# GpSimd forms S5's rotated states itself, and the read-out takes two products of each turn

## What is computed

```python
bu_r = jnp.einsum('bsgc,gpc->bsgp', ug, bbar_r)
bu_i = jnp.einsum('bsgc,gpc->bsgp', ug, bbar_i)
# x[s] = abar * x[s-1] + bu[s], complex, along the sequence
_, _, xr, xi = lax.associative_scan(_complex_affine_combine, ...)
y = (jnp.einsum('bsgp,gcp->bsgc', xr, c_re) - jnp.einsum('bsgp,gcp->bsgc', xi, c_im) + d_skip * ug)
y = jax.nn.gelu(y)
return y * jax.nn.sigmoid(y @ w_glu + b_glu)
```

## Time and profile before

| | |
|---|---|
| Median of 3 runs | 1662.81 us (1662.75 to 1663.93) |
| The profiled execution | 1659.71 us |
| Its span, first to last instruction | 1657.9 us |
| PE busy | 1551.6 us (94%) |
| VectorE (DVE) busy | 1259.0 us (76%) |
| ScalarE (ACT) busy | 1043.8 us (63%) |
| GpSimd (POOL) busy | 62.8 us (4%) |
| DMA | 469.68 MB, mean 283 GB/s |

### The profile page before, as it was taken

The page is one execution under the profiler, slowest core; times in us unless marked ns, Lnnn a source line. Parts: engine busy times, 40 slices in busy tenths (PEclk is TensorE's granted clock), DMA queues, the critical chain, the costliest instruction groups (busy, mean ns, idle before and its releaser), DMA issues.

```text
span 1657.9 us, 22266 instructions
## 1 busy us (share of the span) xinstructions
PE 1551.6 (94%) x7619; PEld 1202.9 (73%) x7620; DVE 1259.0 (76%) x1719; ACT 1043.8 (63%) x1374; POOL 62.8 (4%) x90
## 2 busy tenths in 40 slices
PE   4899989999897888999999999999999999999997
PEld 2545468887764456888888888888888888888885
DVE  6896345443646237989989989989989989989987
ACT  3105444443425626778778778778778778778775
POOL 5251000000000000000000000000000000000000
PEclk9999999999888988999999999999999999999999
DMA  9635855545654837999999999999999999999970
GB/s 319 232 102 195 313 203 200 177 156 177 228 181 150 307 116 265 365 332 358 365 328 364 362 331 366 350 334 362 354 335 363 351 338 362 351 337 364 353 260 27
DMA packets 203752, 469.68 MB, mean 283 GB/s; under 512 B 5108, under 2 KB 11558, under 8 KB 203574
## 3 DMA queue, kind: packets, MB, share of 16 engines
q1 hardware_dynamic: 202656, 466.80, 77.9%
q0 software_dynamic: 400, 1.09, 0.3%
q10 hardware_dynamic: 646, 1.16, 0.2%
HBM read 467.98 MB, written 1.05 MB: 283 GB/s over the span
## 4 chain that ended last, share of the span: by engine, by line
PE 78%; DVE 6%; ACT 5%; issue 2%; DMA 0%; DVEq 0%; ACTq 0%
PE ps L783 22%; PE ps L785 21%; PE ps L784 21%; PE ps L789 2%; PE ps L1330 2%; DVE w_lo L1882 2%; PE ps L1289 2%; PE ps L1056 1%; ACT work L1778 1%; PE ps L808 1%; ACT w_hi L1548 1%; ACT uT L1561 1%; PE ps L828 1%; PE ps L1204 0%; PE ps L1399 0%
## 5 line engine op out<-in xcount | busy, mean ns | idle before, releaser
L1882 DVE TENSOR_TENSOR w_lo<-ring,w_hi 128x1024 fp32r<-128x1024 f32 (+2 forms) x576 | 667.4, 1192 | 116.3 <-ACT w_hi L1548 102.5
L1548 ACT ACTIVATE w_hi<-ring 128x1024 fp32r<-128x1024 f32 (+2 forms) x576 | 594.9, 1038 | 210.3 <-PE ps L785 206.7
L783 PE MATMUL ps<-w_hi,e_hi 128*128 128x512 f32 x896 | 356.6, 398 | 9.7 <-DVE w_lo L1882 9.7
L785 PE MATMUL ps<-w_hi,e_lo 128*128 128x512 f32 x896 | 350.5, 391 | 0.0
L784 PE MATMUL ps<-w_lo,e_hi 128*128 128x512 f32 x896 | 349.6, 390 | 0.0
L1882 DVE TENSOR_TENSOR w_lo<-ring_more,w_hi 128x1024 fp32r<-128x1024 f32 x192 | 228.8, 1220 | 40.5 <-ACT w_hi L1548 38.1
L1548 ACT ACTIVATE w_hi<-ring_more 128x1024 fp32r<-128x1024 f32 x192 | 201.6, 1067 | 70.6 <-PE ps L785 70.6
L783 PEld LDWEIGHTS ps<-w_hi,e_hi 128*128 128x128 f32 x896 | 168.8, 188 | 46.3 <-DVE w_lo L1882 13.2
L785 PEld LDWEIGHTS ps<-w_hi,e_lo 128*128 128x128 f32 x896 | 168.6, 188 | 36.7
L784 PEld LDWEIGHTS ps<-w_lo,e_hi 128*128 128x128 f32 x896 | 169.0, 189 | 33.6
L783 PE MATMUL ps<-w_hi,eT_hi 128*128 128x512 f32 x448 | 176.6, 394 | 5.7 <-DVE w_lo L1882 5.7
(11 more groups left out here) (281 smaller groups left out, 1611.3 us busy)
## 6 DMA issues: line engine op xcount, KB each, us to landing
ring<-in_moe_w_gate SPq DMA_DIRECT2D x48, 2048.0 KB, 10.1
ring<-in_moe_w_up SPq DMA_DIRECT2D x40, 2048.0 KB, 10.3
ring<-in_moe_w_down SPq DMA_DIRECT2D x32, 2048.0 KB, 10.1
ring<-in_w_ada SPq DMA_DIRECT2D x24, 2048.0 KB, 9.1
ring_more<-in_moe_w_down SPq DMA_DIRECT2D x24, 2048.0 KB, 7.9
ring_more<-in_moe_w_up SPq DMA_DIRECT2D x16, 2048.0 KB, 9.8
ring_more<-in_moe_w_gate SPq DMA_DIRECT2D x8, 2048.0 KB, 9.6
ring<-in_ff_w_gate SPq DMA_DIRECT2D x5, 2048.0 KB, 7.8
```

The source lines that it names most:

```text
L783: mm(o, xh, wh, start=start, stop=False)
L785: return mm(o, xl, wh, start=False, stop=stop)
L1548: fn(w, src, ACT.Copy).then_inc(hi_ready, 1)
L1882: V.tensor_tensor(w_lo[0:n, c, 0:f], src, w_hi[0:n, c, 0:f].bitcast(F32), ALU.subtract).then_inc(lo_ready, 1)
```

## The change

GpSimd waits for its two products of a turn and then forms, in place, the difference of the two that make up the rotated state's real part (into `o[:, 0, 0]`) and the sum of the two that make up its imaginary part (into `o[:, 1, 0]`), 128x256 each. The read-out then takes two products of each turn in place of four, with the real part of C and minus its imaginary part. The third set of read-out weights and its copy on ScalarE go, and with it 512 columns of SBUF per partition; the buffers laid out behind it move by as much. The order of the blocks on PE stays.

```diff
-        s5_cT = W0.take(3, 4, P)
+        s5_cT = W0.take(2, 4, P)
...
                 for i in range(2):
-                    w = nc.gpsimd.tensor_tensor(o[:, i], z, phase[:, i, j, :].unsqueeze(1).broadcast_to([P, 2, S]), ALU.mult)
-                w.then_inc(post_ready, 1)
+                    step(nc.gpsimd.tensor_tensor(o[:, i], z, phase[:, i, j, :].unsqueeze(1).broadcast_to([P, 2, S]), ALU.mult))
+                step.wait()
+                nc.gpsimd.tensor_tensor(o[:, 0, 0], o[:, 0, 0], o[:, 1, 1], ALU.subtract)
+                nc.gpsimd.tensor_tensor(o[:, 1, 0], o[:, 1, 0], o[:, 0, 1], ALU.add).then_inc(post_ready, 1)
...
-                    pe.wait_ge(s5_wT_ready, 5)
+                    pe.wait_ge(s5_wT_ready, 4)
...
-                for i, (c, a, b) in enumerate(((0, 0, 0), (1, 1, 1), (2, 1, 0), (2, 0, 1))):
+                for i in range(2):
                     for j in (j0, j0 + 1):
                         r = slice(32 * (j % 4), 32 * (j % 4) + 32)
-                        w = mm(ps[7][r, (t % 2) * S:(t % 2 + 1) * S], s5_cT[:, c, t, r], post[j % 4][:, a, b, :],
-                               start=i == 0, stop=i == 3, tile_position=(0, 32 * (j % 4)))
-                        if i == 3:
+                        w = mm(ps[7][r, (t % 2) * S:(t % 2 + 1) * S], s5_cT[:, i, t, r], post[j % 4][:, i, 0, :],
+                               start=i == 0, stop=i == 1, tile_position=(0, 32 * (j % 4)))
+                        if i == 1:
                             w.then_inc(y_part_done, 1)
...
-                for i, (dst, scale) in enumerate(((s5_bT[:, 0], 1.0), (s5_bT[:, 1], 1.0), (s5_cT[:, 0], 1.0),
-                                                  (s5_cT[:, 1], -1.0), (s5_cT[:, 2], -1.0))):
-                    bank = ps[(5, 6, 7, 7, 4)[i]]
-                    act.wait_ge(s5_padT, (1, 2, 3, 3, 4)[i])
+                for i, (dst, scale) in enumerate(((s5_bT[:, 0], 1.0), (s5_bT[:, 1], 1.0), (s5_cT[:, 0], 1.0), (s5_cT[:, 1], -1.0))):
+                    bank = ps[(5, 6, 7, 4)[i]]
+                    act.wait_ge(s5_padT, i + 1)
```

## The result

The changed kernel takes 1671.1 us, the kernel before 1662.8 (18 runs each): a ratio of 1.0048, 95% interval 1.0039 to 1.0058, so 8.0 us more, between 6.5 and 9.6. The forecast was 1672, and slower.

The account below looks back on a forecast made before the run. VectorE and GpSimd, excluding each other in SBUF, were taken to bound the S5 stage through GpSimd's last turn. +7.5 us delay and +2 clock make +9.5 on the span, 1667.4; carried to the median, 1672 us, range 1667 to 1677.

Parts of the forecast that it names:

- The place: End of the S5 stage: any delay of GpSimd's last turn beyond 0.2 us delays the GLU product and everything behind.
- The mechanism: S5 stage: VectorE instructions with two SBUF inputs and GpSimd ones reading SBUF exclude each other; the later one blocks fully.
- Plain turn with GpSimd behind, 4.76 us: S5 turn: products 2.50, two scans of 0.55, subtraction and addition of 0.58 each, 4.76 in place of 3.71 us.
- The other turns: S5 stage: plain turn after GpSimd caught up 4.25 us, rotary turns 6.27 or 5.72, last turn 5.05.
- The new instructions alone, 0.70 us: GpSimd's subtraction and addition of 128x256 take 0.70 us each where nothing holds them.
- The halved read-out, 0.96 us: PE's read-out of two turns has 4 products in place of 8, so 0.96 us in place of 1.92.
- PE's gain inside the stage is worth nothing: S5 stage: worthless if VectorE and GpSimd become slower than 7.3 us for two turns; only the last read-out counts, -0.96 us.
- The clock, 2 us: PE idles before the GLU product, which may run at half speed and lose up to 3.5 us; 2 taken.
- The sum: +7.5 us at the last read-out's end plus 2 for the clock: +9.5 us on the span of 1657.9, so 1667.4.
- The rival that GpSimd isn't held by the scans: S5 stage: GpSimd's own chain is the bound, 3.9 us per plain turn; +0.3 us, 1663; chance 0.06.
- the one that PE sets the pace: S5 stage: PE is the bound and the halved read-out wins 7.7 us, giving 1655; chance 0.03.
- the one that is worse than the sum: S5 stage: subtraction and addition at 0.79 while held, +5 us, and 3.5 for the clock, also within the stage: 1679; chance 0.05.

Follow-up runs that it names:

- the first two experiments: GpSimd's part alone in the kernel before: ratio 1.0044 to it; read-out's part alone, the changed kernel without subtraction and addition: ratio 0.9980 to the kernel before.

## Why the prediction was right

- *The place.* GpSimd's last turn has no slack: shown. The chain after runs through L763 and L764, and a pure delay there comes back in the time whole, with about 2 us for the clock on top.
- *The mechanism.* Products, scans, subtraction and addition exclude each other: shown by the scans that read PSUM (2.25 us for two become 1.26, and the loss goes) and by the half width (4.58 to 4.05 us).
- *Plain turn with GpSimd behind, 4.76 us.* Measured 4.58. The mis-sized term is the held instruction: 0.58 us from the moment it is let in, taken from L747 in the earlier trace rows. The turn leaves 4.58 - 2.49 = 2.09 us for four pieces, with scans of 0.55 some 0.50 us each. The half width bears it out: 4.05 - 2.50 - 1.10 leaves 0.23 us for each of two instructions of 128 columns, which take 0.46 alone; at either width the held one is 0.23 us shorter. Over eight turns this is 1.4 of the 1.9 us by which GpSimd ended earlier than forecast (142.9, not 144.8).
- *The other turns.* Between the ends of the scans, the profiled execution has 4.25 us for the first turn after the start (forecast 4.25), 5.62 and 6.26 for rotary turns (5.72 and 6.27), 5.00 for the last (5.05). The tail is 4.05 us (138.85 to 142.90; forecast 4.07).
- *The new instructions alone, 0.70 us.* 0.72 to 0.73. The Trainium skill, "GPSIMD Engine Reference", section "3.1 Elementwise — side-by-side cycle accounting", gives about 2.6 cycles per element for two inputs at 1.2 GHz, as an estimate 2.2 ns per column. The runs agree: 1.27 us for 512 columns, 0.73 for 256 and 0.46 for 128 differ by 2.1 ns per column, and about 0.19 us of each doesn't depend on the width.
- *The halved read-out, 0.96 us.* It takes 1.06 to 1.11 us at full clock (in the run with the read-out's part alone) and 1.53 at the end of the changed kernel's stage, mostly at the lower level. So it saves 0.8 to 0.9 us, not 0.96.
- *PE's gain inside the stage is worth nothing.* Right for the change as a whole. Alone, the read-out's part brings the GLU product forward by 2.5 us: about 0.9 us for the last read-out, and the rest from GpSimd's shorter waits for read-outs.
- *The clock, 2 us.* Right in kind, and it fell earlier than thought: the forecast had the GLU product meet it. The changed kernel by stretches, granted clock third from last:

```profile
140.00:143.40 3.40, 0.45 (x4) 0.26 (x6) 2.17 (x10) 1.02 (x3) 2.82 (x4) 1.00 0.83 267
143.40:146.80 3.40, 3.40 (x16) 1.84 (x13) 0.48 (x1) 1.70 (x3) 0.00 (x0) 0.50 0.92 349
146.80:154.00 7.20, 7.08 (x34) 5.99 (x33) 2.23 (x15) 4.28 (x12) 0.00 (x0) 1.00 0.00 0
```

The lower level meets the read-out (+0.5 us against 1.06) and the scores behind it, which end about 0.5 us after PE could have gone on with the GLU product, and only 0.3 us of the GLU product (7.50 and not 7.19). Some 1.3 us in all in this execution.
- *The sum.* +7.5 and 2 for the clock were forecast, 9.5 in all. At the end of the GLU product +7.0 stand, some 5.7 without the clock and 1.3 by it, and +8.0 in the time. So both terms were too large, the first by the held instructions; that the time came nearer to the forecast than the stage did is owed to 1 us that the forecast has nothing for, and so is luck or noise. The profiled execution's span is even 12.3 us longer, and 5.3 of these come after that point: from the end of the GLU product on it took 1516.6 us (1670.2 - 153.57) against 1511.3 before. No run puts this part down to the change: with GpSimd's part alone it is 1511.3 too (1664.8 less 153.5), with a pure delay 1516.7 (1672.7 less 156.0), and the one kernel that was profiled twice, with the scans from PSUM, has 1512.9 and 1509.4. A single profile carries several us of this, so the 1 us between 7.0 and 8.0 can't be placed, and it lies within the interval.

The rival that GpSimd isn't held by the scans is out by its plain turns (4.58, not 3.9); the one that PE sets the pace by the first two experiments; the one that is worse than the sum by the held instructions, which came out shorter and not longer. Its other half, a clock that falls within the stage too, did come true (0.67 and 0.66 above), but cost nothing, since PE wasn't what the stage waited for.

## What to carry to other kernels

An engine's idle share isn't room for work when its instructions exclude those of another: add up the exclusive pieces of one turn of both engines, and if they already fill the turn (here 2.50 + 1.13 of 3.71 us), every added piece lengthens it by nearly all that it takes once it is let in (0.87 us for two pieces of 0.50 here). Before work is moved to GpSimd, see whether VectorE's instructions beside it can take one input from PSUM: here it turned +8 us into -4. It isn't a gain by itself: in the kernel before the same edit cost 4 us. A saving on a third engine that seems worthless may be what such an edit needs, so try the two together.

## What the runs showed of the hardware

- The two engines take turns by single instructions, also between back-to-back instructions of one engine: in a plain turn of the changed kernel each of the two scans waits for a GpSimd instruction, and subtraction and addition each wait for a scan.
- A held GpSimd instruction of 256 columns needs about 0.50 us once it is let in, against 0.73 alone, and one of 128 columns 0.23 us against 0.46: as if 0.23 us of either passed while it waits.
- A scan that has one of its inputs in PSUM isn't held (0.662 to 0.687 us over 32 of them, beside GpSimd's work).
- PE's granted clock went to 0.50 around waits that were often short, and the first matmuls afterwards took up to twice their time (read-out 3.63 against 1.90 us). At the end of the stage the waits were 6.33 and 3.77 us with the pure delays, 3.20 in the changed kernel and 1.98 with the scans from PSUM; within the stage of the changed kernel one of 0.99 us came just before. With GpSimd's part alone the wait at the end, 1.85 us, passed without it (read-out 1.97 us). So the length of the last wait alone doesn't say whether it comes.
